# Which weight blocks of the mixer's input projection go to TensorE as whole fp32, and the convolution's taps dealt out anew

## What is computed

```python
h = x @ w_in                                   # 1024 x 3072
q, f_pre, i_v, g, a, a_gate = jnp.split(h, ...)
f = lb + (1.0 - lb) * jax.nn.sigmoid(f_pre);  k = (1.0 - lb) * jax.nn.sigmoid(-f_pre)
o = hgrn2_chunked(heads(q), heads(k), heads(i_v), heads(jnp.log(f)))   # 4 heads, 8 chunks of 32 tokens
o = rms(o) * hg_norm_g * jax.nn.silu(g)
u = a * jax.nn.sigmoid(a_gate)
u = conv(u, cv_w) + cv_b                       # 31 causal taps per channel, 512 channels
u = jax.nn.silu(layer_norm(u, cv_ln_g, cv_ln_b))
y = jnp.concatenate([o, u], -1) @ w_out
```

## Time and profile before

| | us |
|---|---|
| median of 3 runs (lowest, highest) | 1336.78 (1336.32, 1338.49) |
| the profiled execution: its time | 1337.18 |
| its span in the trace | 1335.4 |
| around the span | 1.8 |
| TensorE busy | 1290.4 (97%) |
| VectorE busy | 858.8 (64%) |
| ScalarE busy | 654.3 (49%) |
| the mixer from in0 to the start of its output projection | 592.72 to 717.59 |

### The profile page before, as it was taken

How to read it: one execution, slowest core, us unless ns; L and a number is a source line. 1 busy time by engine, 2 the same in 40 slices (tenths; PEclk the granted TensorE clock), 3 DMA queues, 4 the chain that set the end, 5 groups by cost and what they waited for, 6 DMA issues and landing times.

```text
span 1335.4 us, 17924 instructions
## 1 busy us (share of the span) xinstructions
PE 1290.4 (97%) x7124; PEld 1118.3 (84%) x7124; DVE 858.8 (64%) x1433; ACT 654.3 (49%) x985; POOL 5.3 (0%) x7
## 2 busy tenths in 40 slices
PE   8999999999999999999989899999999999999997
PEld 7788888997788888899978887888888987788886
DVE  5665557878677665678997655545557664654555
ACT  5544446657464444532725544543445554544443
POOL 0000000000000000000000000000001000000000
PEclk9999999999999999999978999999999999999998
DMA  8555555542455555435423432655554542455551
GB/s 276 179 188 191 188 175 190 183 132 80 134 174 188 189 189 188 159 128 183 161 82 111 157 120 89 207 182 176 189 189 143 174 127 95 158 177 183 186 186 58
DMA packets 61571, 215.84 MB, mean 162 GB/s; under 512 B 6576, under 2 KB 9904, under 8 KB 61232
## 3 DMA queue, kind: packets, MB, share of 16 engines
q1 hardware_dynamic: 61056, 213.15, 48.7%
q10 hardware_dynamic: 432, 1.54, 0.3%
HBM read 213.62 MB, written 1.05 MB: 161 GB/s over the span
## 4 chain that ended last, share of the span: by engine, by line
PE 82%; DVE 11%; ACT 4%; issue 1%; DMA 1%; SPq 0%; DVEq 0%; ACTq 0%
PE bank L1825 24%; PE bank L1827 24%; PE bank L1826 24%; DVE w_lo L1038 3%; PE bank L1847 2%; DVE arena L1642 2%; PE bank L2013 1%; PE bank L1900 1%; ACT w_hi L528 1%; PE bank L2111 1%; PE bank L2151 1%; DMA w_raw<-weights_d 1%; ACT xs L667 1%; PE bank L2122 1%; DVE xs L1711 0%
## 5 line engine op out<-in xcount | busy, mean ns | idle before, releaser
L1038 DVE TENSOR_TENSOR w_lo<-w_raw,w_hi 128x1024 fp32r<-128x1024 f32 x385 | 469.9, 1225 | 370.1 <-ACT w_hi L528 368.7
L528 ACT ACTIVATE w_hi<-w_raw 128x1024 fp32r<-128x1024 f32 x385 | 406.0, 1059 | 525.2 <-PE bank L1827 500.2
L1825 PE MATMUL bank<-w_hi,x_hi 128*128 128x512 f32 (+2 forms) x992 | 372.7, 376 | 11.9 <-DVE w_lo L1038 5.2
L1827 PE MATMUL bank<-w_hi,x_lo 128*128 128x512 f32 (+2 forms) x992 | 367.1, 370 | 0.0
L1826 PE MATMUL bank<-w_lo,x_hi 128*128 128x512 f32 (+2 forms) x992 | 367.0, 370 | 0.0
L1825 PEld LDWEIGHTS bank<-w_hi,x_hi 128*128 128x128 f32 x992 | 187.1, 189 | 47.2 <-issue 9.3
L1827 PEld LDWEIGHTS bank<-w_hi,x_lo 128*128 128x128 f32 x992 | 186.9, 188 | 31.8
L1826 PEld LDWEIGHTS bank<-w_lo,x_hi 128*128 128x128 f32 x992 | 187.2, 189 | 30.2
L1825 PE MATMUL bank<-w_hi,h_hi 128*128 128x512 f32 (+1 forms) x364 | 142.3, 391 | 0.0
L1827 PE MATMUL bank<-w_hi,h_lo 128*128 128x512 f32 (+1 forms) x364 | 141.3, 388 | 0.0
L1826 PE MATMUL bank<-w_lo,h_hi 128*128 128x512 f32 (+1 forms) x364 | 141.3, 388 | 0.0
(11 more groups left out here) (309 smaller groups left out, 1459.4 us busy)
## 6 DMA issues: line engine op xcount, KB each, us to landing
w_raw<-weights_d SPq DMA_DIRECT2D x395, 512.0 KB, 3.3
arena<-weights_d SPq DMA_DIRECT2D x4, 512.0 KB, 5.6
arena<-late_d SPq DMA_DIRECT2D x1, 1056.0 KB, 5.8
xs<-x_d SPq DMA_DIRECT2D x2, 512.0 KB, 6.2
kv_mem<-mem_d ACTq DMA_DIRECT2D x1, 1024.0 KB, 7.6
out_d<-xs SPq DMA_DIRECT2D x4, 256.0 KB, 2.8
cst<-cst_d SPq DMA_DIRECT2D x1, 671.0 KB, 10.6
arena<-pT_d ACTq DMA_DIRECT2D x1, 256.0 KB, 2.6
```

The costliest lines, as they stand in the source:

```text
L528: nc.scalar.activation(w_hi[:, slot(b), :], w_raw[:, b % RAW, :], ACT.Copy).then_inc(hi_ready, 1)
L1038: nc.vector.tensor_tensor(w_lo[:, slot(b), :], w_raw[:, b % RAW, :], w_hi[:, slot(b), :].bitcast(F32), ALU.subtract).then_inc(lo_ready, 1)
L1825: nc.tensor.matmul(out, wh, xh, start=start, stop=False, skip_group_check=True)
L1827: return nc.tensor.matmul(out, wl, xh, start=False, stop=stop, skip_group_check=True)
```

## The change

`WHOLE` had in0 to in9. It now has in0, in1, in10 to in19 and g0 to g3: 16 blocks where there were 10. So in2 to in9 become split, and in10 to in19 and g0 to g3 become whole. A new function multiplies the value blocks whole. The table of the taps is new: 96 taps instead of 90 stand in the twenty stations of the input blocks. The masked scores of VectorE, which stood ahead of station 18, now stand behind station 19.

```diff
-WHOLE = range(FIRST["ab_in"], FIRST["ab_in"] + 10)
+WHOLE = [FIRST["ab_in"] + n for n in (0, 1, *range(10, 24))]
 def parts_of(b):
-    return b + 1 - min(max(b + 1 - WHOLE.start, 0), len(WHOLE))
+    return b + 1 - sum(w <= b for w in WHOLE)
...
-            taps, made, comes = [0] * CC, [0] * CC, (0, 12, 26, 40)
+            taps, made, comes = [0] * CC, [0] * CC, (0, 9, 17, 27)
...
-            beside = {1: 12, 3: 14, 5: 14, 7: 8, 8: 5, 9: 5, 10: 5, 11: 5, 12: 4, 13: 1, 14: 4, 15: 2, 16: 0, 17: 3, 18: 4, 19: 4}
+            beside = (0, 6, 3, 4, 4, 4, 6, 5, 6, 6, 7, 6, 6, 1, 5, 4, 2, 5, 8, 8)
             for n in range(20):
-                if n == 18:
-                    masked_scores()
                 blk()
...
-                conv_taps(beside.get(n, 0))
+                conv_taps(beside[n])
+            masked_scores()
...
+            def whole_values(b, bank, part, x):
+                pe.wait_ge(raw_in[b % RAW], 16 * (b // RAW + 1))
+                for t in range(2):
+                    for k in range(4):
+                        ins = nc.tensor.matmul(bank[:, t * S:(t + 1) * S], x[:, 4 * part + k, 0, t * P:(t + 1) * P],
+                                               w_raw[:, b % RAW, k * S:(k + 1) * S], start=part == 0 and t == 0 and k == 0,
+                                               stop=part == 1 and k == 3, skip_group_check=True)
+                ins.then_inc(block_done, 1)
...
-                if b in WHOLE:
+                if n >= 16:
+                    whole_values(b, PB[4 + 2 * ((n - 16) // 2)], n % 2, xs)
+                elif b in WHOLE:
                     whole_chunk(b, half(4 + n % 4, 0), xs, lambda k: pe.wait_ge(res_ready, k + 1))
-                elif n < 16:
+                else:
                     chunk(b, half(4 + n % 4, 0), x_hi, x_lo, operand(4))
-                elif n >= 16:
-                    values(b, PB[4 + 2 * ((n - 16) // 2)], n % 2, x_hi, x_lo)
...
-                chunk(blk(), half(6 + h % 2, h // 2), x_hi, x_lo)
+                whole_chunk(blk(), half(6 + h % 2, h // 2), xs, lambda k: None)
```

## The result

The changed kernel took 1339.88 us (median of 16 runs, 1335.5 to 1341.7), the kernel before 1336.38 (16 runs, 1335.08 to 1338.49). The ratio is 1.0023, 95% interval 1.0016 to 1.0029: slower by 3.5 us, where +3.5 was forecast. The changed kernel's runs lie nearly twice as far apart as those of before (6.2 us from lowest to highest, 3.4 before).

What follows compares the result with a forecast made beforehand. TensorE, busy 1290.4 of 1335.4 us, bounds the page, VectorE the stage from scores to first head. Shifts accumulate to +3.5 at the output projection: span 1338.9, plus 1.8 around it, less 0.4, gives 1340.3 us; range 1335.0 to 1344.0.

Steps and rivals of the forecast that it cites:

- in10 starts: Start of the first later whole input block: 625.7 against 627.07, -1.4 us, after short stops among the split blocks.
- scores start: Scores after in10 to in19: ten whole blocks, 34.5 us without a stop, start at 660.2 against 656.80, +3.4.
- first state parts: TensorE's work behind VectorE's masked scores: starts at 667.2, not 664.58, +2.6, after 21 taps and 2.5 us of masked scores.
- Prices: Each whole block costs TensorE 0.56 us more, six 3.4; six saved splits relieve VectorE of 6.8 us.
- Front: Input blocks up to in10: TensorE waits 0.35 us at in0's eighth tile, 1.0 and 1.5 for gated products.
- The walk: Following the four queues in time order through the mixer with the measured durations; output projection came out 3.5 us later.
- Loads: A whole block's buffer reloads only when TensorE is done, about 3.4 us to landing; delays in5, m0 and m2.
- o0 to the end of g2: Head loop: output and state parts end at 679.3, g2 takes 5.1 us partly at low clock, ending at 684.4.
- the rival of the relief at its face: m0 and m2 hold up no states; saved splits 6.8 and taps 1.4 against 3.4 on TensorE: -4, 1332.8; 7%.
- Tail: Last transposes lose their 1.43 us wait for taps; 1.8 us of low clock taken back; output projection at 721.1, +3.5.
- The rival of a clock that stays up: Clock doesn't fall ahead of o0; g2 takes 3.45 us, output projection at 715.7, -1.9, or 1334.9 us; 14%.
- Two gates at half clock: Head loop: g2 and g3 both run at 1.2 GHz throughout, some +7 us, 1343.8; 20%.

Runs made afterwards that it cites:

- the reordered kernel before: The kernel before with only the splits of m0 to m3 moved behind the states, ScalarE's copies likewise; 1334.05 us, ratio 0.9982.

## Why the prediction was right

The stages ahead of the mixer were 1.05 us shorter in the execution after (in0 at 591.67, not 592.72). That is not the change's doing: in the traces of the other kernels in0 starts between 591.39 and 592.32, the reordered kernel before at 592.25. So I compare distances from in0's start, step by step.

| step | predicted | traced |
|---|---|---|
| in10 starts | -1.4 | 32.89 - 34.35 = -1.5 |
| scores start | +3.4 | 67.43 - 64.08 = +3.4 |
| first state parts | +2.6 | 74.58 - 71.86 = +2.7 |
| o0 | +1.7 | 81.72 - 80.54 = +1.2 |
| o2 | +4.6 | 101.50 - 97.38 = +4.1 |
| o3 | +6.5 | 111.29 - 104.64 = +6.7 |
| m1 | +5.3 | 115.83 - 111.07 = +4.8 |
| output projection | +3.5 | 127.10 - 124.87 = +2.2 |

- *Prices.* Ten whole blocks took 34.54 us; the row's 0.56 us more per block held, not the 0.96 that the prediction estimated from the count of passes on the Trainium skill's page "FP8 and Floating Point Precision".
- *Front.* The stops came where they were put, 0.81 and 1.08 for 1.0 and 1.5; 0.21 for the 0.35 ahead of in0's last tiles. The walk had each a little too long.
- *Loads.* in5's copy began at 603.08, 3.0 us after ScalarE was free for it; VectorE waited 3.52 us before m0's split (about 4 forecast) and 5.09 before m2's (3 to 5). The move of the splits behind the states shows that these waits cost: 10.2 us less with the same work. The stop ahead of o0 was 2.78 us, 3.6 forecast.
- *o0 to the end of g2.* Here two terms were off and cancelled. The walk let the clock fall ahead of o0, as before, and gave the output and the state parts 4.3 us and g2 5.1. In the trace the clock was still full when o0 began and fell 1.4 us later; output and state parts took 3.9 us, g2 5.7. The sums are 9.4 and 9.6.
- *Two slips in the sums.* o2 at 694.7 and 9 us behind it give 703.7 for o3, not 703.9; and the rival of the relief at its face comes to 3.4 - 6.8 - 1.4 = -4.8, not -4. Neither decides anything.
- *Tail.* The taps' wait went. The last stage took 11.27 us, 2.5 less than before, where I took back 1.8: in this execution the clock was back at 702, before m1. Those 0.7 us are the largest part of the 1.3 us by which the traced step is below +3.5. The stage behind the output projection kept its length (617.9 us, 617.8 before).
- *The balance.* From in0 to m1 TensorE's stops were 9.8 us before and 9.6 after: the relief took away those ahead of scores, transposes and last taps, and the loads put others in their place. The clock was low for 20.5 us up to the output projection before and for 17.1 after. So the relief and the late loads about cancel, and the traced +2.2 is the price of the six whole blocks, 3.4 us, less what the clock gave back.
- *Rivals.* The rival of a clock that stays up hung on whether the clock falls ahead of o0. It did not, and yet g2 ran slow, since it fell 1.4 us behind o0's start; the prediction had named the wrong moment to look at. That rival's time, 1334.9, is close to the shortest of the 16 runs, 1335.5. No trace of that run exists, but its mean granted clock was 0.991, the highest of the 16; it was 0.989 or 0.990 in the six runs from 1337.5 to 1339.1 and 0.984 in the longest (1341.7). That fits the rival as what some runs are, and does not show it. Two gates at half clock were not seen: g3 took its 3.45 us. The relief at its face value (1332.8) did not come with the waits in front; with the waits behind the states the same blocks gave 1329.64, clock included.

The mechanism was right: dearer blocks, a relief that late loads use up, and where they stand. That the median lies at exactly the forecast +3.5 is partly luck: the traced step was +2.2, steps of the walk were off by up to 1.3 us, and single runs of this kernel lie up to 6.2 us apart.

## What to carry to other kernels

When work is taken off one engine by keeping a buffer longer on another, cost the load that starts later, and look up what stands behind the wait for it in every in-order queue: the same blocks in the same kernel were 3.5 us slower or 6.8 faster than before, by where the wait stood. A wait removed at one place is not a gain until the next late item is named; moving only m2's split gained nothing. And a table of filler work belongs to one set of waits: with the old table the new blocks cost 7.6 us more, and dealing the taps out once more, with the masked scores ahead of station 19, gave the last 6 to 7.

## What the runs showed that I had not expected

Where TensorE has long stops, runs of one kernel differ by the clock that they were granted: 1335.5 us at a mean of 0.991 to 1341.7 at 0.984 for the changed kernel, 1334.02 at 0.993 to 1344.41 at 0.986 with twelve filler matmuls. In the kernel before (1335.08 to 1338.49 us) the two hardly go together, and with hardly a stop four runs lay between 1322.1 and 1324.95. Filling a stop of 2.8 us moved the fall of the clock from 674.8 to 682.7 instead of preventing it, so that the low stretch lay under the next whole block, and in these traces that decided which load was late. The clock can also fall behind a stop: in the changed kernel it was full through the stop of 2.78 us ahead of o0 and fell 1.4 us after TensorE had begun again.
